# HGRN operand sums moved to the first head's levels 0 and 1, and input units 4 and 5 run as a tenth pair

## The chip, the cores and the metric

One core of a Trainium2 chip runs the kernel. The metric is the device time of one execution in microseconds (us), told as the median of several. TensorE, VectorE (DVE in the profile), ScalarE (ACT), GpSimd (POOL) and SyncE (SP) run their own instruction streams and meet at semaphores.

## The reference

The reference is two blocks in a row on x of 1024 tokens by 1024. The part around the change is the first block's HGRN2 mixer:

```python
h = _rmsnorm(x, norm_mix[layer])
proj = h @ w_in                          # 1024 x 4096: q, f, i, g
q, f, i, g = jnp.split(proj, 4, axis=-1)
log_f = jnp.logaddexp(jnp.log(lb), jnp.log1p(-lb) + jax.nn.log_sigmoid(ff))
k = (1.0 - lb) * jax.nn.sigmoid(-ff)
qf = jax.nn.silu(q.astype(jnp.float32)) * (HGRN_HEAD_DIM ** -0.5)
o = _hgrn2_chunk_scan(heads(qf), heads(k), heads(i.astype(jnp.float32)), heads(log_f))
o = o * lax.rsqrt(jnp.mean(o * o, axis=-1, keepdims=True) + NORM_EPS)
```

The scan has 8 heads of 128. An output projection, a squared-relu MLP (1024 to 4096 and back), a second block with retention and a convolution, and a second MLP follow. All in float32.

## The kernel before, in words

Each matrix product in float32 is made of three fp32r matmuls: weights and activations are both split into a rounded high part and a low rest, and hi x hi, hi x lo and lo x hi are added (`tiles`, L1052 to L1054; 128x512 each). A *unit* is 128 output columns of a projection, for 1024 tokens in two halves; a plain unit is 2 halves x 8 k-tiles x 3 = 48 matmuls. Head n owns units 3n (v), 3n+1 (f, later k) and 3n+2 (q). The weights of a unit (512 KB) come through one of two slots of `w_raw`; SP loads the next unit into a slot once `w_split` says the slot's last low part is made.

From unit 6 on two units run as a *pair* (`paired`): one Strassen-Winograd step over the first four k-tiles. Seven products of 6 matmuls (P1, P5, P2, S2xT2, S4xB22, S3xT3, A22xT4) and four plain rests of 12 over k-tiles 4 to 7 make 90 matmuls. The operand sums T1, T3, T2, T4 of the activations serve all pairs of the stage: VectorE makes each (`in1_combine`, L2296, two instructions), ACT rounds it (`in1_high`, L3232), VectorE makes the low part (`in1_low`, L2303). For the weights of a pair ACT rounds the raw upper half (`in_high_raw`, L3151), POOL adds S1 and S2 (L926, L928), ACT rounds them (`in_high_s12`, L3157), POOL makes low parts (`split_paired`, L910, counted by `in1_parts`), rounds and splits the rest tiles (L914, L917), and adds S3 and S4; ACT rounds these (`in_high_more`). ACT copies P1, P5 and the partial sums U2, U3 from PSUM (`in_copy`, L3128), and VectorE adds them to the banks (L1933, L1920). A table of PSUM banks (`PAIR_BANKS1`) says in which of four banks each pair works, and with it which eviction each product waits for. TensorE's first product of a pair waits for `in1_parts`:

```python
                part(1)
                free(n_u)
                seventh(b_u, A11, B11, True).then_inc(s.prod, 1)
                part(3)
```

Between the pieces of a unit or pair TensorE does the side work of the heads ahead (`hgrn_steps`). For the head before the current units it makes levels L0 to L6, and for the one before that L7, the turns of v and k, the states and the output. A level goes around three engines: VectorE multiplies q and k by the decay (`grow`, L2079, with the next decay L2080) once TensorE has made that level, and takes the scores (L2103); ACT mixes q and k into one operand for the next level (`gather`, L3175, L3176); TensorE multiplies (L1192). The key turn (L1111, second use) waits for level 7's multiply and for its scores.

The order on every engine is written by hand: `hgrn_iteration` on VectorE, `second_iteration`, `even_iteration` and `odd_iteration` on ACT, the calls at the end of POOL's part. In iteration 1 (units 3 to 5, head 0's levels) VectorE makes the four operand sums after levels 2 to 5 and the low parts after level 5 and at the end; ACT rounds the first pair's weights after it has mixed for level 6.

## Time and profile before

| what | value |
|---|---|
| median of 3 runs | 2258.19 us (2257.88 to 2261.65) |
| the profiled execution | 2260.37 us |
| its span, first to last instruction | 2258.6 us |
| TensorE busy, matmuls | 2244.6 us, 99% of the span |
| VectorE busy | 1682.2 us, 74% |
| POOL busy | 1256.8 us, 56% |
| ACT busy | 951.9 us, 42% |
| mean granted TensorE clock | 0.998 |
| HBM traffic | 121 GB/s over the span |

A timeline row gives the start and the length of an instruction; matmuls overlap, so their pace is the distance of their starts. "[idle before <-releaser]" is how long the engine had stood still, and what it waited for.

### The profile page before, as it was taken

How to read it: one execution, taken by the hardware profiler on the slowest of the kernel's cores; microseconds unless marked ns; L12 is line 12 of the kernel's file. 1: busy time of each engine (PE TensorE's matmuls, PEld its weight loads, DVE VectorE, ACT ScalarE, POOL GpSimd, SP SyncE). 2: the span in 40 equal slices, each digit the busy share in tenths (PEclk: the TensorE clock that was granted, in tenths of full speed). 3: DMA queues.
4: the chain of work that ended last, by engine and by line, in shares of the span. 5: the costliest groups of instructions: out<-in, count | busy, mean ns of one | idle time of the engine just before them, and what ended most of it. 6: DMA issues, size and time to landing. Idle time of an engine off the chain costs nothing.

```text
span 2258.6 us, 32472 instructions
## 1 busy us (share of the span) xinstructions
PE 2244.6 (99%) x10744; PEld 1879.4 (83%) x10744; DVE 1682.2 (74%) x2355; ACT 951.9 (42%) x1565; POOL 1256.8 (56%) x1420
## 2 busy tenths in 40 slices
PE   9999999999999999999999999999999999999998
PEld 7888888888888888888888888888888888888887
DVE  7887887856878777876666877765787787787766
ACT  6355544424634533543432224322453454344433
POOL 4544552344556566655546666763556665666562
PEclk9999999999999999999999999999999999999999
DMA  4011111023264556455313111112335645554553
GB/s 158 29 38 38 33 34 47 29 93 130 94 229 144 180 173 214 149 177 187 114 55 121 66 43 41 48 56 103 121 136 181 214 148 177 186 198 142 196 198 140
DMA packets 60020, 274.46 MB, mean 122 GB/s; under 512 B 7184, under 2 KB 10384, under 8 KB 42000
## 3 DMA queue, kind: packets, MB, share of 16 engines
q1 hardware_dynamic: 58800, 270.51, 34.5%
q10 hardware_dynamic: 1120, 2.65, 0.3%
q8 instruction: 58, 0.95, 0.2%
q14 instruction: 42, 0.34, 0.0%
HBM read 211.27 MB, written 61.87 MB: 121 GB/s over the span
## 4 chain that ended last, share of the span: by engine, by line
PE 95%; DVE 3%; DVEq 1%; ACT 0%; issue 0%; DMA 0%; SPq 0%; ACTq 0%; POOL 0%; POOLq 0%
PE prod_ps L1466 8%; PE prod_ps L1467 8%; PE prod_ps L1468 8%; PE side_ps L1467 7%; PE side_ps L1468 7%; PE side_ps L1466 7%; PE prod_ps L1052 7%; PE prod_ps L1054 7%; PE prod_ps L1053 7%; PE prod_ps L1343 3%; PE prod_ps L1345 3%; PE prod_ps L1344 3%; PE prod_ps L1333 3%; PE prod_ps L1331 3%; PE prod_ps L1332 3%; PE side_ps L1192 2%
## 5 line engine op out<-in xcount | busy, mean ns | idle before, releaser
L1052 PE MATMUL prod_ps<-operand_hi,w_hi 128*128 128x512 f32 x696 | 275.3, 396 | 2.1 <-DVE operand_lo L1971 2.1
L1054 PE MATMUL prod_ps<-operand_hi,w_lo 128*128 128x512 f32 x696 | 271.8, 391 | 0.0
L1053 PE MATMUL prod_ps<-operand_lo,w_hi 128*128 128x512 f32 x696 | 271.4, 390 | 0.0
L842 POOL TENSOR_TENSOR w_lo<-w_raw,w_hi 128x256 fp32r<-128x256 f32 x168 | 154.8, 941 | 127.4 <-ACT w_hi L3410 127.1
L842 POOL TENSOR_TENSOR w_lo<-w_s,w_hi 128x256 fp32r<-128x256 f32 x168 | 129.0, 771 | 143.0 <-ACT w_more_hi L3418 115.1
L797 POOL CAST w_hi<-w_raw 128x1024 fp32r<-128x1024 f32 x41 | 43.6, 1064 | 266.6 <-PE prod_ps L1054 177.2
L2491 DVE TENSOR_TENSOR x_res<-prod_ps,x_res 128x512 f32<-128x512 f32 x130 | 89.0, 685 | 97.6 <-PE prod_ps L1468 97.6
L801 POOL TENSOR_TENSOR w_lo<-w_raw,w_hi 128x256 fp32r<-128x256 f32 x164 | 155.5, 979 | 3.3
L1052 PEld LDWEIGHTS prod_ps<-operand_hi,w_hi 128*128 128x128 f32 x696 | 131.1, 188 | 29.1 <-DVE operand_lo L1971 2.4
L1054 PEld LDWEIGHTS prod_ps<-operand_hi,w_lo 128*128 128x128 f32 x696 | 130.9, 188 | 27.9
L1053 PEld LDWEIGHTS prod_ps<-operand_lo,w_hi 128*128 128x128 f32 x696 | 131.2, 189 | 26.2
L3410 ACT ACTIVATE w_hi<-w_raw 128x512 fp32r<-128x512 f32 x114 | 70.7, 628 | 184.2 <-PE side_ps L1468 78.7
L2491 DVE TENSOR_TENSOR x_res<-side_ps,x_res 128x512 f32<-128x512 f32 x182 | 122.5, 684 | 27.4 <-PE side_ps L1468 23.3
L3414 ACT ACTIVATE w_hi<-w_s 128x512 fp32r<-128x512 f32 x114 | 72.0, 632 | 166.4 <-DVE w_s L2375 166.4
L1343 PE MATMUL prod_ps<-operand_hi,w_hi 128*128 128x512 f32 x320 | 128.4, 401 | 0.0
L1345 PE MATMUL prod_ps<-operand_hi,w_lo 128*128 128x512 f32 x320 | 125.8, 393 | 0.0
L1344 PE MATMUL prod_ps<-operand_lo,w_hi 128*128 128x512 f32 x320 | 125.4, 392 | 0.0
L842 POOL TENSOR_TENSOR w_s_lo<-w_s,w_more_hi 128x256 fp32r<-128x256 f32 x168 | 123.7, 757 | 0.0
L2476 DVE TENSOR_TENSOR wino_lo<-wino,wino_hi 128x1024 fp32r<-128x1024 f32 x78 | 109.0, 1410 | 11.3 <-ACT wino_hi L3481 9.3
L3418 ACT ACTIVATE w_more_hi<-w_s 128x512 fp32r<-128x512 f32 x114 | 71.9, 633 | 83.7 <-DVE w_s L2385 83.7
L842 POOL TENSOR_TENSOR w_a_lo<-w_raw,w_more_hi 128x256 fp32r<-128x256 f32 x84 | 67.4, 803 | 38.1 <-ACT w_more_hi L3421 38.1
L2375 DVE TENSOR_TENSOR w_s<-w_s,w_raw 128x256 f32<-128x256 f32 x114 | 79.3, 695 | 8.5
(461 smaller groups left out, 6842.8 us busy)
## 6 DMA issues: line engine op xcount, KB each, us to landing
w_raw<-stream SPq DMA_DIRECT2D x202, 512.0 KB, 3.6
x_park<-x_res SPq DMA_DIRECT2D x45, 1024.0 KB, 8.1
x_res<-x_park SPq DMA_DIRECT2D x45, 1024.0 KB, 6.8
swapped<-op_park SPq DMA_DIRECT2D x39, 1024.0 KB, 5.0
op_park<-swapped SPq DMA_DIRECT2D x6, 1024.0 KB, 8.2
x_in<-x_t SPq DMA_DIRECT2D x16, 256.0 KB, 5.2
x_res<-x_t SPq DMA_DIRECT2D x8, 512.0 KB, 4.3
end_park<-x_res SPq DMA_DIRECT2D x4, 1024.0 KB, 3.8
```

The lines of the kernel that those rows point to most:

```text
L801: low = nc.gpsimd.tensor_tensor(w_lo[:, slot, ks], w_raw[:, slot, ks], w_hi[:, slot, ks].bitcast(F32), ALU.subtract)
L842: return nc.gpsimd.tensor_tensor(dst, src, high.bitcast(F32), ALU.subtract)
L1052: nc.tensor.matmul(into, w_h, a_h, start=(k == 0), stop=False)
L1053: nc.tensor.matmul(into, w_h, a_l, start=False, stop=False)
L1054: last = nc.tensor.matmul(into, w_l, a_h, start=False, stop=(k == KT - 1))
L1343: nc.tensor.matmul(into, w_h, a_h, start=first, stop=False, skip_group_check=not start)
L1344: nc.tensor.matmul(into, w_h, a_l, start=False, stop=False, skip_group_check=not start)
L1345: mm = nc.tensor.matmul(into, w_l, a_h, start=False, stop=k == KT - 1, skip_group_check=not start)
L1466: nc.tensor.matmul(into, w_h, a_h, start=first and kk == 0, stop=False, skip_group_check=not first)
L1467: nc.tensor.matmul(into, w_h, a_l, start=False, stop=False, skip_group_check=not first)
L1468: mm = nc.tensor.matmul(into, w_l, a_h, start=False, stop=kk == 1, skip_group_check=not first)
L2491: nc.vector.tensor_tensor(x_res[:, m, tokens(half)], src, x_res[:, m, tokens(half)], ALU.add).then_inc(down_taken, 1)
```

## The change

`U_PAIRED1` goes from `U_IN1 + 6` to `U_IN1 + 4`: units 4 and 5 become pair 0 and there are ten pairs. The bank table gets other last entries. On TensorE iteration 1 is now `second_head`: unit 3 as two plain halves, followed by L0 and L1, then the new pair with L2 to L6 between its pieces. VectorE makes all four sums between level 0 and level 1, the low parts directly behind level 1, and takes level 6's scores ahead of its multiply. ACT has a new order for this iteration, and the first copies of the later heads' iterations lose their special case. POOL no longer splits units 4 and 5 singly.

```diff
-U_PAIRED1 = U_IN1 + 6
+U_PAIRED1 = U_IN1 + 4
-PAIR_BANKS1, PAIR_FREED1 = pair_banks(U_PAIRED1, IN1_PAIRS, [(0, 1, 3, 2), (1, 3, 2, 0), (3, 2, 0, 1)])
+PAIR_BANKS1, PAIR_FREED1 = pair_banks(U_PAIRED1, IN1_PAIRS, [(1, 0, 2, 3), (3, 2, 0, 1)])
...
-            split_units(4, U_PAIRED1)
...
+                if n == 1:
+                    mids = [None, None, lambda: newer_level(2), lambda: newer_level(3), None, None]
+                    ends = [lambda: newer_level(0), lambda: newer_level(1), None, lambda: newer_level(4),
+                            lambda: newer_level(5), lambda: newer_level(6)]
+                elif n >= HEADS1 or n < 1:
...
+            def second_head():
+                mids, ends = hgrn_steps(1, 1)
+                for half in range(NH):
+                    product(3, 1, half, 0, mid=mids[half])
+                    ends[half]()
+                in1_pair(0, mids[2:6], ends[2:6])
...
-                    scores_first = number == LEVELS - 2 and 2 <= n < HEADS1
+                    scores_first = number == LEVELS - 2 and 1 <= n < HEADS1
...
+                if n == 1:
+                    newer_level(0)
+                    in1_combine(T1, 0, 1, T1)
+                    group(0)
+                    in1_combine(T3, 2, 1, T3)
...
+                    newer_level(1)
+                    in1_low(T1, 1)
+                    group(1)
...
+                    newer_level(5)
+                    group(4)
+                    group(5)
+                    newer_level(6)
+                    second(4)
+                    second(5)
+                    return
...
             def second_iteration():
                 newer_gather(1, 1)
+                in1_high(T1, 1)
+                in1_high(T3, 2)
+                in1_high(T2, 3)
                 newer_gather(1, 2)
...
                 in_high_raw(in1, 0)
                 in_high_s12(in1, 0)
...
+                newer_gather(1, 4)
+                f_sigmoids(1, 1)
+                in_high_raw(in1, 1)
+                in_high_s12(in1, 1)
+                newer_gather(1, 5)
+                copy_u3(in1, 0)
+                q_sigmoid(1, 0)
+                newer_gather(1, 6)
```

VectorE, from level 0's scores of head 0 on, before (`in_t_200`, `_206`, `_203`, `_207` are T1, T3, T2, T4; `hgrn_kq_78` is head 0's keys and queries, `_79` head 1's):

```order
L2091 TENSOR_TENSOR hgrn_scores_80<-side_ps,ident 128x1024
L1957 TENSOR_TENSOR hgrn_v_t_77<-prod_ps,inv_rms 128x512 [waits prod]
L2079 TENSOR_TENSOR hgrn_kq_78<-hgrn_kq_78,hgrn_f 128x2x512 [waits side_done]
L2080 TENSOR_TENSOR hgrn_decay_83<-hgrn_f 128x512
L2103 COPY_PREDICATED hgrn_scores_80<-masks,side_ps 128x4x64 x2
L1957 TENSOR_TENSOR hgrn_v_t_77<-prod_ps,inv_rms 128x512 [waits prod]
L2079 TENSOR_TENSOR hgrn_kq_78<-hgrn_kq_78,hgrn_decay_83 128x2x256x2 [waits side_done]
L2080 TENSOR_TENSOR hgrn_decay_84<-hgrn_decay_83 128x256
L2103 COPY_PREDICATED hgrn_scores_80<-masks,side_ps 128x4x32x2 x2
```

and with the change:

```order
L2103 TENSOR_TENSOR hgrn_scores_80<-side_ps,ident 128x1024
L2321 SCALAR_TENSOR_TENSOR in_t_200<-x_in,gain,in_t_200 128x512 [waits in1_scaled]
L2321 SCALAR_TENSOR_TENSOR in_t_200<-x_in,gain,in_t_200 128x512
L1969 TENSOR_TENSOR hgrn_v_t_77<-prod_ps,inv_rms 128x512 [waits prod]
L2321 SCALAR_TENSOR_TENSOR in_t_206<-x_in,gain,in_t_206 128x512 x2
L2321 SCALAR_TENSOR_TENSOR in_t_203<-x_in,gain,in_t_200 128x512 x2
L2321 SCALAR_TENSOR_TENSOR in_t_207<-x_in,gain,in_t_203 128x512 x2
L2091 TENSOR_TENSOR hgrn_kq_78<-hgrn_kq_78,hgrn_f 128x2x512 [waits side_done]
L2092 TENSOR_TENSOR hgrn_decay_83<-hgrn_f 128x512
L2115 COPY_PREDICATED hgrn_scores_80<-masks,side_ps 128x4x64 x2
L2328 TENSOR_TENSOR in_t_lo<-in_t_200,in_t_hi 128x1024 [waits in1_t_high]
```

The four sums now stand between level 0's scores and level 1's multiply (`hgrn_kq_78<-hgrn_kq_78,hgrn_f 128x2x512`), which came directly behind the v eviction before.

ACT, from the first rounding of a sum to the roundings of the first pair's weights (`w_hi<-w_raw`, `w_hi<-w_s`) before; `hgrn_mixed` rows are two per level, and the ones for levels 4 and 5 (`16x16`, `8x32`) and 6 are told apart by their shapes:

```order
L3232 ACTIVATE in_t_hi<-in_t_200 128x1024 [waits in1_t_made]
L3175 ACTIVATE hgrn_mixed<-hgrn_kq_78 128x16x16 [waits level_fed]
L3176 ACTIVATE hgrn_mixed<-hgrn_kq_78 128x16x16
L3221 ACTIVATE hgrn_f<-hgrn_kq_79 128x512 [waits evac]
L3222 ACTIVATE hgrn_kq_79<-hgrn_kq_79 128x2x2x128
L3224 ACTIVATE hgrn_f<-hgrn_f,lb 128x512
L3232 ACTIVATE in_t_hi<-in_t_206 128x1024 [waits in1_t_made]
L3175 ACTIVATE hgrn_mixed<-hgrn_kq_78 128x8x32 [waits level_fed]
L3176 ACTIVATE hgrn_mixed<-hgrn_kq_78 128x8x32
L3151 ACTIVATE w_hi<-w_raw 128x512 [waits prod,w_landed0]
L3157 ACTIVATE w_hi<-w_s_0_121 128x512 [waits in1_sum]
L3232 ACTIVATE in_t_hi<-in_t_203 128x1024 [waits in1_t_made]
```

and with the change, from the mixing for level 1 on:

```order
L3200 ACTIVATE hgrn_mixed<-hgrn_kq_78 128x256 [waits level_fed]
L3201 ACTIVATE hgrn_mixed<-hgrn_kq_78 128x256
L3257 ACTIVATE in_t_hi<-in_t_200 128x1024 [waits in1_t_made]
L3257 ACTIVATE in_t_hi<-in_t_206 128x1024 [waits in1_t_made]
L3257 ACTIVATE in_t_hi<-in_t_203 128x1024 [waits in1_t_made]
L3200 ACTIVATE hgrn_mixed<-hgrn_kq_78 128x128x2 [waits level_fed]
L3201 ACTIVATE hgrn_mixed<-hgrn_kq_78 128x128x2
L3176 ACTIVATE w_hi<-w_raw 128x512 [waits prod,w_landed0]
L3182 ACTIVATE w_hi<-w_s_0_121 128x512 [waits in1_sum]
L3257 ACTIVATE operand_hi<-in_t_207 128x2x512 [waits in1_t_made,prod]
L3153 ACTIVATE in_c_213<-prod_ps 128x512 [waits in1_prod]
```

The first pair's weights are now rounded behind the mixing for level 2 (`128x128x2`) instead of behind that for level 6 (`8x32`), and that mixing stands behind the rounding of three sums.

## Rows read from the trace of the kernel before

**Rows 1.** The page: its first line and the busy times.

```profile
span 2258.6 us, 32472 instructions
...
PE 2244.6 (99%) x10744; PEld 1879.4 (83%) x10744; DVE 1682.2 (74%) x2355; ACT 951.9 (42%) x1565; POOL 1256.8 (56%) x1420
```

**Rows 2.** Waits of TensorE over the whole span, the longest.

```profile
PE side_ps L1111 <- DVE hgrn_scores L2103: 2.1, 1, 2.1
```

**Rows 3.** Timeline of TensorE: start us, us, engine, line, operation [idle before <-releaser].

```profile
42.49 0.39 PE L1054 MATMUL prod_ps<-operand_hi,w_lo 128*128 128x512 f32 x1
...
50.65 0.40 PE L1054 MATMUL prod_ps<-operand_hi,w_lo 128*128 128x512 f32 x1
...
58.98 0.48 PE L1052 MATMUL prod_ps<-operand_hi,w_hi 128*128 128x512 f32 x1
```

**Rows 4.** Timeline of TensorE around the key turn of head 0.

```profile
99.58 0.96 PE L1111 MATMUL side_ps<-ident,hgrn_kq 128*128 128x128 f32 x7 [2.15 <-DVE hgrn_scores L2103]
...
100.61 0.63 PE L1344 MATMUL prod_ps<-operand_lo,w_hi 128*128 128x512 f32 x1
...
104.02 0.39 PE L1343 MATMUL prod_ps<-operand_hi,w_hi 128*128 128x512 f32 x1
```

**Rows 5.** Windows: busy us of each engine, PEclk, DMA share, GB/s.

```profile
8.60:12.00 3.40, 3.32 (x8) 2.65 (x9) 2.75 (x5) 2.85 (x6) 3.32 (x4) 0.52 1.08 395
...
100.00:104.00 4.00, 4.00 (x14) 3.21 (x13) 3.34 (x4) 1.76 (x5) 2.20 (x4) 0.57 0.72 232
```

**Rows 6.** Timeline of TensorE near the start.

```profile
8.68 0.80 PE L1052 MATMUL prod_ps<-operand_hi,w_hi 128*128 128x512 f32 x1 [1.93 <-DVE operand_lo L1971]
...
11.83 0.40 PE L1053 MATMUL prod_ps<-operand_lo,w_hi 128*128 128x512 f32 x1
```

**Rows 7.** Timeline of VectorE.

```profile
54.01 1.22 DVE L2091 TENSOR_TENSOR hgrn_scores<-side_ps,ident 128x1024 f32<-128x1024 f32 x1
...
59.26 1.33 DVE L2079 TENSOR_TENSOR hgrn_kq<-hgrn_kq,hgrn_f 128x1024 f32<-128x1024 f32 x1 [3.25 <-PE side_ps L1192]
...
67.48 1.41 DVE L2296 SCALAR_TENSOR_TENSOR in_t<-x_in,gain,in_t 128x512 f32<-128x512 f32 x2
...
71.68 1.89 DVE L2296 SCALAR_TENSOR_TENSOR in_t<-x_in,gain,in_t 128x512 f32<-128x512 f32 x2
...
80.72 0.78 DVE L2103 COPY_PREDICATED hgrn_scores<-masks,side_ps 128x256 f32<-128x256 uint8 x2
...
94.56 1.75 DVE L2303 TENSOR_TENSOR operand_lo<-in_t,operand_hi 128x1024 fp32r<-128x1024 f32 x1
...
96.23 1.76 DVE L2079 TENSOR_TENSOR hgrn_kq<-hgrn_kq,hgrn_decay 128x1024 f32<-128x1024 f32 x1
...
99.60 0.69 DVE L1933 TENSOR_TENSOR in_c<-prod_ps,in_c 128x512 f32<-128x512 f32 x1 [0.16 <-issue]
```

**Rows 8.** Timeline of ACT.

```profile
60.63 0.44 ACT L3175 ACTIVATE hgrn_mixed<-hgrn_kq 128x256 f32<-128x256 f32 x1 [5.74 <-DVE hgrn_kq L2079]
...
60.97 0.43 ACT L3176 ACTIVATE hgrn_mixed<-hgrn_kq 128x256 f32<-128x256 f32 x1
...
67.60 0.64 ACT L3221 ACTIVATE hgrn_f<-hgrn_kq 128x512 f32<-128x512 f32 x1 [1.78 <-DVE hgrn_kq L2136]
...
68.82 0.82 ACT L3224 ACTIVATE hgrn_f<-hgrn_f,lb 128x512 f32<-128x512 f32 x1
...
81.21 0.61 ACT L3151 ACTIVATE w_hi<-w_raw 128x512 fp32r<-128x512 f32 x1
...
83.20 0.61 ACT L3213 ACTIVATE sig<-hgrn_kq 128x512 f32<-128x512 f32 x1
```

**Rows 9.** Timeline of POOL.

```profile
58.48 1.04 POOL L797 CAST w_hi<-w_raw 128x1024 fp32r<-128x1024 f32 x1 [8.15 <-issue]
...
81.90 1.89 POOL L910 TENSOR_TENSOR w_lo<-w_raw,w_hi 128x256 fp32r<-128x256 f32 x2 [7.74 <-ACT w_hi L3151]
```

**Rows 10.** The page, section 6: loads of weights.

```profile
w_raw<-stream SPq DMA_DIRECT2D x202, 512.0 KB, 3.6
```

More of the change, by code:

```diff
@@ L1258, in sixth_level_then_back @@
                     back()
-                if n >= HEADS1 or n < 2:
+                if n == 1:
[3 more added lines that the diff above has]
+                elif n >= HEADS1 or n < 1:
                     mids = [turn_v_and_last_level, turn_k, kv_then_second_level, lambda: newer_level(3), None,
@@ L1287, in hgrn_iteration, with in1_pair @@
                         ends[j]()
+            def in1_pair(j, mids, ends):
+                m0, m1, m2, m3 = mids
+                e0, e1, e2, e3 = ends
+                paired(in1, j, {"P2": m0, "c11": e0, "P6": m1, "c12": e1, "P7": m2, "c22": e2, "P4": m3, "c21": e3})
+            def second_head():
[4 more added lines that the diff above has]
+                in1_pair(0, mids[2:6], ends[2:6])
             def two_heads(n):
@@ L1293, in two_heads @@
                 for p in range(3):
-                    m0, m1, m2, m3 = mids[4 * p:4 * p + 4]
-                    e0, e1, e2, e3 = ends[4 * p:4 * p + 4]
-                    paired(in1, (3 * n - U_PAIRED1) // 2 + p,
-                           {"P2": m0, "c11": e0, "P6": m1, "c12": e1, "P7": m2, "c22": e2, "P4": m3, "c21": e3})
+                    in1_pair((3 * n - U_PAIRED1) // 2 + p, mids[4 * p:4 * p + 4], ends[4 * p:4 * p + 4])
             def in_weight(s, which, kk):
@@ L1440, in _ @@
             hgrn_iteration(0, 0, mid_start=True)
-            hgrn_iteration(1, 1)
+            second_head()
             for n in range(2, HEADS1, 2):
@@ L2178, in first_pair_of @@
                     first_two(in1, (unit - U_PAIRED1) // 2)
+                if n == 1:
[3 more added lines that the diff above has]
+                    in1_combine(T3, 2, 1, T3)
+                    dve.drain()
+                    in1_combine(T2, 2, 1, T1)
+                    dve.drain()
+                    in1_combine(T4, 2, 0, T2)
+                    newer_level(1)
+                    in1_low(T1, 1)
+                    group(1)
+                    in1_low(T2, 3)
+                    in1_low(T3, 3)
+                    in1_low(T4, 4)
+                    newer_level(2)
+                    group(2)
+                    newer_level(3)
+                    first_pair_of(u + 1)
+                    group(3)
+                    newer_level(4)
+                    newer_level(5)
[5 more added lines that the diff above has]
+                    return
                 if 2 <= n < HEADS1:
@@ L2285, in hgrn_iteration @@
                 second(5)
-                if n == 1:
-                    in1_low(T2, 3)
-                    in1_low(T3, 3)
-                    in1_low(T4, 4)
             def in1_combine(op, m, half, other):
@@ L3255, in second_iteration @@
                 newer_gather(1, 1)
+                in1_high(T1, 1)
+                in1_high(T3, 2)
+                in1_high(T2, 3)
                 newer_gather(1, 2)
-                newer_gather(1, 3)
-                f_sigmoids(1, 0)
-                newer_gather(1, 4)
-                in1_high(T1, 1)
-                newer_gather(1, 5)
-                f_sigmoids(1, 1)
-                in1_high(T3, 2)
-                newer_gather(1, 6)
                 in_high_raw(in1, 0)
                 in_high_s12(in1, 0)
-                in1_high(T2, 3)
-                q_sigmoid(1, 0)
-                newer_gather(1, LEVELS - 1)
-                q_sigmoid(1, 1)
-                take_v(2)
                 act.wait_ge(prod, 2 * U_PAIRED1)
                 in1_high(T4, 4)
+                copy_p1(in1, 0)
+                copy_p5(in1, 0)
+                newer_gather(1, 3)
+                in_high_more(in1, 0)
+                f_sigmoids(1, 0)
+                copy_u2(in1, 0)
+                newer_gather(1, 4)
[6 more added lines that the diff above has]
+                newer_gather(1, 6)
+                in_high_more(in1, 1)
+                q_sigmoid(1, 1)
+                newer_gather(1, LEVELS - 1)
             def even_iteration(n, j):
@@ L3277, in even_iteration @@
                 copy_p5(in1, j)
-                if n > 2:
-                    take_v(n)
-                else:
-                    in_high_more(in1, j)
+                take_v(n)
                 in_high_raw(in1, j + 1)
@@ L3340, in _ @@
             for n in range(2, HEADS1, 2):
-                even_iteration(n, 3 * (n // 2 - 1))
-                odd_iteration(n + 1, 3 * (n // 2 - 1) + 2)
+                even_iteration(n, 3 * (n // 2) - 2)
+                odd_iteration(n + 1, 3 * (n // 2))
             def gate_sigmoid(j):
```

11 lines of the change are left out of this document (removed).

## The prediction

> **What bounds the kernel now.** I read the page first: TensorE is busy for 2244.6 of 2258.6 us [rows 1]. So the time is TensorE's instruction stream plus its few gaps, and a gap of a few us anywhere reaches the end whole. The view of the waits names the largest gap: 2.1 us, once [rows 2]. TensorE's timeline gives the rest. Its pace: 36 matmuls of 512 columns from 42.49 to 50.65 us, 0.2267 us each; unit 4 starts at 58.98 [rows 3]. The gap: it ends at 99.58, where the key turn (k) inside the first pair waits for VectorE. After it, eight matmuls from 100.61 to 104.02 take 0.426 us each [rows 4], and the windows give a granted clock of 0.57 from 100 to 104 us: the 1.2 GHz level [rows 5]. They cost 3.41 - 8 x 0.2267 = 1.6 us on top of the gap. The same had followed a gap of 1.93 us at 8.68 [rows 6], with a clock of 0.52 [rows 5]. So a gap of some 2 us costs nearly twice its length here.
>
> A change is told from no change on this kernel only beyond 0.2%, 4.5 us. Everything below happens before 110 us; behind that the pairs follow one another as before.
>
> **The change, part by part.**
>
> *Fewer matmuls.* Units 4 and 5 took 4 halves x 8 tiles x 3 = 96 matmuls; a pair takes 7 products x 6 + 4 x 12 = 90. Six go: -6 x 0.2267 = **-1.4 us**. Level products (L1, L2, ...) and turns keep their number.
>
> *The first weights of the new pair come late.* This is the term that decides. TensorE's first product P1 needs w_lo, which POOL makes behind the ACT rounding w_hi<-w_raw. In ACT's new order that rounding stands behind the mixing for level 2, which waits for VectorE's level-1 multiply (the kq grow, L2079 before). In VectorE's new order this multiply stands behind all four operand sums. Link by link: VectorE is done with level 0 at 55.23. Then four sums of two instructions, 1.41 us each while POOL idles, and one eviction of 0.69: 6.3 us end on end, some 0.3 less as neighbours overlap by 0.07, 0.2 more for two drains: 61.5. The multiply takes 1.33 [rows 7]: 62.8. ACT mixes in 0.77 (60.63 to 61.40) and rounds in 0.61 [rows 8]: 64.2. POOL's first low part takes 0.95, half of 1.89 [rows 9]: **65.2**. TensorE wants it at 58.98, so it waits **6.2 us**. Before, the same split was covered by two units of matmuls. The least this can be is VectorE having finished the sums in 5.3 us (eight instructions spaced 0.6, plus the eviction): 5.5; the most is contention on the sums, below: 8.2.
>
> VectorE's sums cost 1.41 a pair with POOL idle and 1.89 with POOL at work (67.48 against 71.68) [rows 7]. By the Trainium skill, GPSIMD Engine Reference, section Specifications, the two engines share their SBUF interfaces, and VectorE instructions with two SBUF inputs contend; these sums are such. If that held here too, they would take 7.6 instead of 5.6, and this term would be 8.2. POOL stood idle for 8.15 us up to 58.48 [rows 9]; now its queue waits at the first low part from about 48 until 64.2, so I take 6.2.
>
> *The clock behind that gap.* A gap three times as long as the two seen surely leaves TensorE at the half clock. The two stretches after a restart were 3.15 us (8.68 to 11.83, seven matmuls) [rows 6] and 3.41 us after 0.7 us of turns. Half of such a stretch is lost: 1.6 at least; the restart may fall early between two changes and cost up to twice that, 3.3. I take **+2.0**; the first 0.4 of it covers the wait for the third weight part (POOL: two more low parts behind the first, 67.0), which I therefore don't add.
>
> *Two small waits further in.* With P1 at 65.3, TensorE would reach the third product's end about 81.2, L5 at 81.2 + 0.9 (L4) + 18 x 0.2267 = 86.2. L5 needs its mixing, which on ACT stands behind the sigmoids of unit 4's second half and the next pair's two roundings: eviction on VectorE 2 x 0.7 to 83.0, sigmoids 2.04 (67.60 to 69.64), roundings 1.15, mixing 0.8 [rows 7, 8]: 87.0. Wait **0.8**. L6 is wanted 4.1 us (18 matmuls) after L5. It needs: VectorE's level-5 multiply 1.23 to 1.75, decay and scores 1.0, an eviction in two steps 1.57, ACT's q sigmoid 0.61 (now ahead of that mixing) and the mixing 0.8: 5.5 with the drains. Wait **1.4**. Both are bounded below by 0 (other work earlier than I put it) and above by 1.8 and 2.0 (POOL beside VectorE all the way: 0.5 more for each multiply). L3 and L4 are ready 0.4 to 0.7 early by the same count. Between the first and last link I take 2.2 together.
>
> *The old gap goes.* It came from VectorE: three low parts of the operand sums, the last at 94.56, stood ahead of the level-7 multiply (96.23), whose scores the turn waits for [rows 2, 7]. These now come about 25 us earlier. By my count level 7's scores end 3 us before the turn is reached. -2.2 for the gap, -1.6 for its half clock: **-3.8 us**.
>
> *What I cost at nothing.* The single split of units 4 and 5 leaves POOL (5 instructions each, off the path). Four ACT copies at 0.55 us and four VectorE additions at 0.69 to 1.1 are added; they lie beside matmuls, save those counted for L5 and L6. The load of unit 6 now waits for the pair's last low part, about 79.7, and needs 3.6 [rows 10]: 83.3, ahead of its rounding at 85.1; were that cover gone, L5 would be late by the difference. The new bank table lets the first product of the last two pairs wait for the second eviction of the pair ahead where it waited for the third, and no wait stood there: 0.
>
> Sum: -1.4 + 6.2 + 2.0 + 2.2 - 3.8 = **+5.2 us**. The profiled execution took 2260.37 for its span of 2258.6; it would take 2265.6. The median of the runs shown is 2258.19, 2.2 lower, so I forecast 2263.4.
>
> **The rivals.**
>
> 1. *The small waits trip the clock as well.* L6's 1.4 us follows L5's 0.8. For it: 1.93 us sufficed at 8.68. Against: no wait of 0.5 to 1.4 in this trace is followed by slow matmuls. Another +1.6: 2265.0. Chance 0.2.
> 2. *The late waits are covered.* Should ACT or VectorE be earlier than I count, or the clock be back soon, the two small waits fall to 0: 5.2 - 2.2 = +3.0, 2261.2, inside what counts as no change. For it: the slow matmuls after P1 give the other engines slack. Against: both chains start from TensorE's own progress and so move with it. Chance 0.22.
> 3. *The first weights are in time* (the other side). Should the rounding reach POOL by 58, the change is -1.4 - 3.8 = -5.2 us: 2253.0, faster by 0.23%. It decides at the P1 chain: its 6.2 us must shrink under 0.7 for a gain of 4.5. Against: the level-1 multiply alone waits for L1, that ends after 58.98, and 1.33 + 0.77 + 0.61 + 0.95 follow it, so 3.7 us remain even with no sum ahead. It needs my reading of ACT's order to be wrong. Chance 0.04.
> 4. *The old gap stays.* If VectorE is still behind at level 7, the -3.8 is missing: +9.0, 2267.2. For it: L6's scores, its multiply and the q scaling now all lie close ahead of level 7. Against: 3 us of slack. Chance 0.05.
> 5. *POOL contends with the sums or the multiplies:* +2 us, 2265.4. Chance 0.07.
>
> **How the numbers follow.** The forecast keeps 0.42, with its own range of +4.0 to +6.6 from the clock term (1.6 to 3.3) and the first chain (5.5 upward); about 0.3 of its 0.42 lies above 4.5. Slower by over 0.2%: 0.3 + 0.2 + 0.05 + 0.07 = 0.62. Within: 0.12 + 0.22 = 0.34. Faster: 0.04. The range runs from 2260.5 (rival 2 with a cheap restart) to 2267.2 (rival 4), leaving out rival 3 and the tails.
>
> **What would show it.** In the profile after: a gap of about 6 us on TensorE ahead of the first paired product, released by POOL's w_lo, from about 59 to 65; 0.43 us a matmul for some 4 us behind it; gaps near 1 us at the fifth and sixth levels of the first head, released by ACT's mixing; no wait at the first key turn, and full pace behind it. The pair behind the new one would start about 94, against 85.5. I am wrong if P1 starts before 62, if TensorE is at full clock right behind it, or if a new wait shows in a later pair.

## The result, and the profile after

The changed kernel takes 2271.14 us (median of 6 runs, 2269.64 to 2271.74); the kernel before, run beside it, 2259.04 (6 runs, 2257.6 to 2261.65). The ratio is 1.005, 95% interval 1.0039 to 1.0061: slower, by more than twice the 5.2 us that were forecast, and above the range given. The profiled execution took 2269.92 us. Of all executions told of in this document one, of 5870.88 us (in e12), was disturbed; without it that median moves by 0.01 us.

The page of the changed kernel, its first line and the busy times:

```profile
span 2268.1 us, 32491 instructions
...
PE 2246.6 (99%) x10738; PEld 1877.4 (83%) x10738; DVE 1684.0 (74%) x2359; ACT 955.9 (42%) x1573; POOL 1264.3 (56%) x1427
```

Against [rows 1] six matmuls are gone (x10738), and still TensorE is busy 2.0 us longer: a matmul at half clock counts as busy for its whole, longer time. Its waits (us in total, times, longest):

```profile
PE prod_ps L1343 <- POOL w_lo L910: 6.3, 2, 5.8
PE side_ps L1191 <- ACT hgrn_mixed L3201: 2.5, 2, 1.9
...
PE prod_ps L1478 <- ACT stage L3518: 1.4, 2, 0.9
```

The wait of [rows 2] is not in the list. The timeline of TensorE from L0 of head 0 (`x16`) to L0 of head 2, with L1, P1, P5, L2, L3, L5, L6, the matmuls behind L6, and the key turn:

```profile
49.98 1.95 PE L1104 MATMUL side_ps<-hgrn_kq 128*128 128x128 f32 x16
...
57.22 1.07 PE L1191 MATMUL side_ps<-hgrn_kq,hgrn_mixed 128*128 128x128 f32 x8
64.07 0.79 PE L1343 MATMUL prod_ps<-operand_hi,w_hi 128*128 128x512 f32 x1 [5.79 <-POOL w_lo L910]
...
67.56 0.50 PE L1343 MATMUL prod_ps<-in_t_hi,w_hi 128*128 128x512 f32 x1 [0.56 <-POOL w_lo L910]
...
70.45 1.07 PE L1191 MATMUL side_ps<-hgrn_kq,hgrn_mixed 128*128 128x128 f32 x8
...
76.23 1.05 PE L1191 MATMUL side_ps<-hgrn_kq,hgrn_mixed 128*128 128x128 f32 x8
...
87.01 1.16 PE L1191 MATMUL side_ps<-hgrn_kq,hgrn_mixed 128*128 128x128 f32 x8 [0.61 <-ACT hgrn_mixed L3201]
...
94.21 1.88 PE L1191 MATMUL side_ps<-hgrn_kq,hgrn_mixed 128*128 128x128 f32 x8 [1.91 <-ACT hgrn_mixed L3201]
95.74 0.77 PE L1343 MATMUL prod_ps<-operand_hi,w_hi 128*128 128x512 f32 x1
...
97.95 0.39 PE L1345 MATMUL prod_ps<-operand_hi,w_lo 128*128 128x512 f32 x1
...
108.58 0.93 PE L1110 MATMUL side_ps<-ident,hgrn_kq 128*128 128x128 f32 x7
...
153.04 1.95 PE L1104 MATMUL side_ps<-hgrn_kq 128*128 128x128 f32 x16
```

The key turn at 108.58 has no gap [rows 4]. P1 waited 5.79 us. L6 waited 1.91, and its eight matmuls took 1.88 in place of 1.05: the clock had fallen there too, as the windows show (PEclk is the third number from the right):

```profile
65.00:70.00 5.00, 4.44 (x16) 2.99 (x15) 5.00 (x5) 1.19 (x2) 4.92 (x4) 0.79 0.00 0
...
95.00:100.00 5.00, 5.00 (x21) 4.23 (x20) 3.75 (x6) 1.98 (x5) 4.71 (x6) 0.71 0.34 103
```

The chain of the first weights, on VectorE, ACT and POOL in turn:

```profile
56.35 4.41 DVE L2321 SCALAR_TENSOR_TENSOR in_t<-x_in,gain,in_t 128x512 f32<-128x512 f32 x6
60.68 1.22 DVE L2091 TENSOR_TENSOR hgrn_kq<-hgrn_kq,hgrn_f 128x1024 f32<-128x1024 f32 x1
```

```profile
62.59 0.61 ACT L3176 ACTIVATE w_hi<-w_raw 128x512 fp32r<-128x512 f32 x1
```

```profile
63.28 2.50 POOL L910 TENSOR_TENSOR w_lo<-w_raw,w_hi 128x256 fp32r<-128x256 f32 x2 [16.81 <-ACT w_hi L3176]
```

This run started 0.9 us earlier (L0 at 49.98, before at 50.88), so these rows are the forecast chain of 61.5, 62.8, 64.2 and 65.2, less 0.9, to within 0.3.

**Two stretches hold the whole difference.** From L0 of head 0 to L0 of head 2 the kernel before took 145.58 - 50.88 = 94.70 us, the changed one 153.04 - 49.98 = 103.06: **+8.4**, forecast +5.2. From there to the last sums of `x_res` on VectorE it is 2105.45 before (2251.03) and 2107.50 after (2260.54): **+2.05**, forecast 0. Inside the second stretch, the kernel before, VectorE and then TensorE in the second MLP:

```profile
1648.94 0.43 DVE L2373 TENSOR_TENSOR w_s<-w_raw 128x256 f32<-128x256 f32 x1 [0.20 <-PE prod_ps L1654]
1649.44 0.43 DVE L2375 TENSOR_TENSOR w_s<-w_s,w_raw 128x256 f32<-128x256 f32 x1
```

```profile
1673.91 0.49 PE L1466 MATMUL prod_ps<-xop_hi,w_hi 128*128 128x512 f32 x1 [0.48 <-ACT stage L3489]
```

and the changed kernel:

```profile
1656.49 0.42 DVE L2398 TENSOR_TENSOR w_s<-w_raw 128x256 f32<-128x256 f32 x1 [0.20 <-PE prod_ps L1666]
1657.34 0.94 DVE L2400 TENSOR_TENSOR w_s<-w_s,w_raw 128x256 f32<-128x256 f32 x1 [0.43 <-issue]
```

```profile
1682.33 0.49 PE L1478 MATMUL prod_ps<-xop_hi,w_hi 128*128 128x512 f32 x1 [0.93 <-ACT stage L3518]
```

VectorE halts for 0.43 us on nothing that the profile shows, the next sum takes 0.94 in place of 0.43, and TensorE's wait at 1682 us is 0.45 longer. No instruction of the change is near.

### The profile page after: what moved, and what is told of

Read it like the earlier page. It is cut to its first block, busy times and chain, and to the rows that moved or that the text cites. A ratio compares the mean times of both kernels' runs of the same rounds, so it can differ in the third digit from the quotient of the medians.

```text
span 2268.1 us, 32491 instructions
## 1 busy us (share of the span) xinstructions
PE 2246.6 (99%) x10738; PEld 1877.4 (83%) x10738; DVE 1684.0 (74%) x2359; ACT 955.9 (42%) x1573; POOL 1264.3 (56%) x1427
## 4 chain that ended last, share of the span: by engine, by line
PE 93%; DVE 3%; DVEq 1%; ACT 1%; issue 1%; SPq 0%; DMA 0%; POOL 0%; ACTq 0%
PE prod_ps L1478 8%; PE prod_ps L1480 8%; PE prod_ps L1479 8%; PE side_ps L1478 7%; PE side_ps L1480 7%; PE side_ps L1479 7%; PE prod_ps L1051 6%; PE prod_ps L1053 6%; PE prod_ps L1052 6%; PE prod_ps L1355 3%; PE prod_ps L1357 3%; PE prod_ps L1356 3%; PE prod_ps L1343 3%; PE prod_ps L1345 3%; PE prod_ps L1344 3%; PE side_ps L1191 2%
## 5 line engine op out<-in xcount | busy, mean ns | idle before, releaser
L1051 PE MATMUL prod_ps<-operand_hi,w_hi 128*128 128x512 f32 x664 | 261.9, 394 | 1.2 <-DVE operand_lo L1983 1.0
L1053 PE MATMUL prod_ps<-operand_hi,w_lo 128*128 128x512 f32 x664 | 258.9, 390 | 0.0
L1052 PE MATMUL prod_ps<-operand_lo,w_hi 128*128 128x512 f32 x664 | 258.4, 389 | 0.0
L842 POOL TENSOR_TENSOR w_lo<-w_raw,w_hi 128x256 fp32r<-128x256 f32 x168 | 154.3, 938 | 128.7 <-ACT w_hi L3439 128.4
L801 POOL TENSOR_TENSOR w_lo<-w_raw,w_hi 128x256 fp32r<-128x256 f32 x156 | 147.9, 978 | 3.1
L1051 PEld LDWEIGHTS prod_ps<-operand_hi,w_hi 128*128 128x128 f32 x664 | 124.7, 188 | 28.0 <-POOL w_lo L995 1.4
L1053 PEld LDWEIGHTS prod_ps<-operand_hi,w_lo 128*128 128x128 f32 x664 | 124.6, 188 | 26.5
L1052 PEld LDWEIGHTS prod_ps<-operand_lo,w_hi 128*128 128x128 f32 x664 | 124.8, 188 | 24.9
L1355 PE MATMUL prod_ps<-operand_hi,w_hi 128*128 128x512 f32 x336 | 134.3, 400 | 0.0
L1357 PE MATMUL prod_ps<-operand_hi,w_lo 128*128 128x512 f32 x336 | 131.4, 391 | 0.0
L1356 PE MATMUL prod_ps<-operand_lo,w_hi 128*128 128x512 f32 x336 | 130.9, 390 | 0.0
L926 POOL TENSOR_TENSOR w_s<-w_raw 128x256 f32<-128x256 f32 x21 | 16.8, 802 | 125.1 <-PE prod_ps L1345 117.2
```

Of the source, the lines that this page charges most:

```text
L801: low = nc.gpsimd.tensor_tensor(w_lo[:, slot, ks], w_raw[:, slot, ks], w_hi[:, slot, ks].bitcast(F32), ALU.subtract)
L842: return nc.gpsimd.tensor_tensor(dst, src, high.bitcast(F32), ALU.subtract)
L1051: nc.tensor.matmul(into, w_h, a_h, start=(k == 0), stop=False)
L1052: nc.tensor.matmul(into, w_h, a_l, start=False, stop=False)
L1053: last = nc.tensor.matmul(into, w_l, a_h, start=False, stop=(k == KT - 1))
L1355: nc.tensor.matmul(into, w_h, a_h, start=first, stop=False, skip_group_check=not start)
```

## The experiments

Called "head" is the stretch from L0 of head 0 to L0 of head 2, "far" the one from there to the last `x_res` sums; "ratio" is to the kernel before, run beside each; it comes from all the times, so it is not always the quotient of the two medians.

**e1, first weights ahead of the mixing for level 2.** Theory A: the gap at P1 is the chain sums, multiply, mixing, rounding, low part.

```diff
             def second_iteration():
+                in_high_raw(in1, 0)
+                in_high_s12(in1, 0)
                 newer_gather(1, 1)
...
-                in_high_raw(in1, 0)
-                in_high_s12(in1, 0)
```

> The changed kernel with ACT's two roundings of the new pair's weights moved ahead of the mixing for level 1, nothing else. Theory A (the gap is a VectorE chain, and the weights are only its first victim): P1 starts at once, but its second product P5 then waits for T1's low part, which VectorE makes behind level 1. In the changed kernel that low part ended at 65.2 and P5 began at 67.56, so the gap moves to P5, stays near 5.5 us, and 2.3 us come off: about 2268.8. Rival B (the late weights are the whole cause): the gap of 5.8, the 0.56 behind it and the half clock of 1.3 to 2 all go, 7.7 to 8.4 us less: about 2263.

Measured: 2272.12 us, ratio 1.0055 (1.0039 to 1.007). P1 has no gap, the second product has it all, and VectorE's six sums take 5.83 us in place of 4.41, since POOL now works beside them. TensorE, then VectorE:

```profile
69.26 0.77 PE L1343 MATMUL prod_ps<-in_t_hi,w_hi 128*128 128x512 f32 x1 [8.25 <-DVE in_t_lo L2328]
```

```profile
57.80 5.83 DVE L2321 SCALAR_TENSOR_TENSOR in_t<-x_in,gain,in_t 128x512 f32<-128x512 f32 x6
63.55 1.74 DVE L2091 TENSOR_TENSOR hgrn_kq<-hgrn_kq,hgrn_f 128x1024 f32<-128x1024 f32 x1
```

ACT's order does set P1's gap, but VectorE's low part of T1 stands right behind it. That is theory A in kind and not in size: the gap grew to 8.25 where 5.5 was expected, and the time did not fall. By the Trainium skill, GPSIMD Engine Reference, section Specifications, POOL contends on the SBUF interfaces with VectorE's instructions of two SBUF inputs; the trace agrees: POOL works from 58.78 us on, each sum takes 0.47 us more, and the multiply 1.74 in place of 1.22.

**e2, all three engines reordered** (T1, T2 and T1's low part ahead of level 1, T3 later, T4's low part on POOL, ACT in the order of need):

```diff
-                    in1_combine(T3, 2, 1, T3)
                     dve.drain()
                     in1_combine(T2, 2, 1, T1)
                     dve.drain()
-                    in1_combine(T4, 2, 0, T2)
+                    in1_low(T1, 1)
                     newer_level(1)
-                    in1_low(T1, 1)
+                    in1_combine(T4, 2, 0, T2)
+                    dve.drain()
+                    in1_low(T2, 2)
                     group(1)
...
```

> The changed kernel with its orders rebuilt: T1, T2 and T1's low part ahead of level 1, T4, T2's low part and T3 behind it, T4's low part on POOL, the weights' roundings first on ACT, mixings ahead of roundings and sigmoids. Theory A (all of the loss is order, none is the pair itself): at most a wait of 0.8 before L3 and 1.1 before S3xT3 stay; relative to the kernel before -1.4 - 3.8 + 1.9 = -3.3 us, about 2255.7. Rival B (ten pairs cost by themselves in head 1, whatever the order): a gap over 3 us stays in the new pair and the time stays above that of the kernel before, 2259 to 2262.

Measured: 2268.47 us, ratio 1.0039 (1.0025 to 1.0053), head 102.29. No gap at P1; instead five: 1.52 at S2xT2, 0.77 and 1.19 at L3 and L4, 1.07 at S3xT3, and the largest at A22xT4, where I had put ACT's copy of U3 behind two roundings:

```profile
90.79 0.79 PE L1350 MATMUL prod_ps<-operand_hi,in_more_hi 128*128 128x512 f32 x1 [4.10 <-ACT in_c L3163]
```

Theory A is out, and rival B came true, with a time above its 2259 to 2262.

**e3, the two later mixings first.**

```diff
-                in_high_raw(in1, 1)
-                in_high_s12(in1, 1)
                 newer_gather(1, 5)
+                in_high_raw(in1, 1)
+                in_high_s12(in1, 1)
                 copy_u3(in1, 0)
-                q_sigmoid(1, 0)
                 newer_gather(1, 6)
+                q_sigmoid(1, 0)
```

> The changed kernel with ACT's mixing for level 5 ahead of the next pair's two roundings and the mixing for level 6 ahead of the q sigmoid. Theory A: the waits before L5 (0.61) and L6 (1.91) go, and with the latter the slow matmuls behind it (1.7, eight level matmuls and five of 512 columns): -4.2 us, about 2267, clock 1.00 from 95 to 100. Rival B (the clock behind L6 is a late echo of the 6 us gap, not of the 1.9 us one): the waits go, 2.5 us, but 95 to 100 stays slow: about 2268.6.

Measured: 2266.10 us, ratio 1.0028 (1.0018 to 1.0039), head 100.10. L5 and L6 start without a wait, all is at full clock behind them, and P1's gap is unchanged:

```profile
65.23 0.79 PE L1343 MATMUL prod_ps<-operand_hi,w_hi 128*128 128x512 f32 x1 [5.79 <-POOL w_lo L910]
...
68.71 0.80 PE L1343 MATMUL prod_ps<-in_t_hi,w_hi 128*128 128x512 f32 x1 [0.56 <-POOL w_lo L910]
...
94.13 1.05 PE L1191 MATMUL side_ps<-hgrn_kq,hgrn_mixed 128*128 128x128 f32 x8
```

The small waits and what followed them were worth 5.0 us by the medians, not 2.2. The head stretch alone would say 3.0, since this trace lost more elsewhere: behind the same wait of 5.79 us, 15 matmuls were slow (P5 took 0.80 in place of 0.50), and from L1 to L2 it took 15.13 us where the changed kernel's trace has 13.23.

**e4, the kernel before with T3's and T4's low parts behind level 7.**

```diff
                 if n == 1:
                     in1_low(T2, 3)
-                    in1_low(T3, 3)
-                    in1_low(T4, 4)
...
                     level(par, LEVELS - 1)
+                    if n == 2:
+                        in1_low(T3, 3)
+                        in1_low(T4, 4)
```

(Level 0 of the next head goes ahead of the first eviction there.)

> The kernel before, without the tenth pair: the low parts of T3 and T4 moved behind head 0's level 7 on VectorE, and level 0 of head 1 ahead of the eviction of v. Theory A (the old gap is these low parts, and its half clock costs as much again): the gap of 2.15 at the key turn and the 1.6 behind it go, -3.8 us, about 2255.2. Rival B (the half clock behind it is not due to the gap): only -2.15, about 2256.9. Rival C (the parts are merely late elsewhere): a wait at S3xT3 takes the place, no change.

Measured: 2257.88 us, ratio 0.9995 (0.9986 to 1.0004), head 92.45. The old gap and its slow matmuls are gone, and a new wait shows at L3 of head 1:

```profile
115.40 1.16 PE L1192 MATMUL side_ps<-hgrn_kq,hgrn_mixed 128*128 128x128 f32 x8 [1.29 <-ACT hgrn_mixed L3181]
```

**e5, the kernel before with 11 more drains on VectorE at the start.** Theory B for the far loss: it comes from where VectorE's instructions lie in its stream.

```diff
                 nc.vector.tensor_tensor(gain[:, G_END1_MIX2], gain[:, G_END1], gain[:, G_MIX2], ALU.mult)
-                dve.drain()
+                for _ in range(12):
+                    dve.drain()
```

> The kernel before with 11 more drains on VectorE among the masks and gains made at the start, far off the path; VectorE's stream gets as long as in the changed kernel (2571 instructions in place of 2560), and nothing else differs. Theory B (the loss of 1.2 to 2.1 us behind the first head, in the second MLP, comes from where VectorE's instructions lie in its stream, not from the pair): the VectorE row pair that takes 0.94 us in place of 0.43 near 1650 us shows here too, the later wait of TensorE at L1466 behind it is 0.9 in place of 0.5 us, and the time is 1.2 to 2.1 us above that of the kernel before, ratio 1.0005 to 1.001. Rival (it comes from the ten pairs themselves, by their banks or the later state of the queues): the stretch from the first head to the end is as in the kernel before, within 0.3 us, ratio 1.000.

Measured: 2261.61 us against 2260.16, ratio 1.0005 (0.9996 to 1.0014), which does not separate them. The trace does: head 94.87, as before, and far 2107.07 (before 2105.45, after 2107.50), with the same halt, then the same wait, and a second halt at 2153.88 us:

```profile
1649.04 0.43 DVE L2374 TENSOR_TENSOR w_s<-w_raw 128x256 f32<-128x256 f32 x1 [0.20 <-PE prod_ps L1654]
1649.89 0.94 DVE L2376 TENSOR_TENSOR w_s<-w_s,w_raw 128x256 f32<-128x256 f32 x1 [0.42 <-issue]
...
2153.88 0.98 DVE L2386 TENSOR_TENSOR w_s<-w_raw,w_s 128x256 f32<-128x256 f32 x1 [0.45 <-issue]
```

```profile
1674.90 0.49 PE L1466 MATMUL prod_ps<-xop_hi,w_hi 128*128 128x512 f32 x1 [0.92 <-ACT stage L3490]
```

These two places hold nearly all of it. Matmul by matmul, TensorE here runs 0.11 us behind the kernel before at 1645 us and 1.01 behind at 1676, then 1.04 at 2152 and 1.62 at 2156. The changed kernel and e3 lose the same two amounts there, 0.85 to 0.9 and 0.6.

**e6, e3 with 5 more drains there** (the same edit to `range(6)`).

> As e3 (ten pairs, the mixings for levels 5 and 6 ahead of the roundings), with 5 more drains on VectorE at the start, far off the path: its stream then has 2576 instructions, 16 more than the kernel before, where e3 has 11 more. e5 showed that 11 drains alone cost 1.6 us behind the first head. Theory B in its narrow form (what counts is where the pair of w_s rows lies within a block of 16 instructions of the stream): the rows near 1650 us take 0.43 us again, the wait behind them 0.5, and the stretch from the first head's end to the last instruction falls back from 2108.4 to about 2107, so the time is 1.2 to 1.5 us under e3's 2266.1. Rival (any added instruction, or another period): the rows stay at 0.94 us or another place is hit, 2108 to 2109 for the stretch, and the time is e3's.

Measured: 2265.75 us, ratio 1.0027 (1.0016 to 1.0039). Far is 2105.70, as before the change (e3: 2106.88), and the halt now meets an instruction three rows earlier:

```profile
1651.48 0.69 DVE L2497 SCALAR_TENSOR_TENSOR stage<-stage,side_ps 128x512 f32<-128x512 f32 x1 [0.43 <-issue]
...
1653.22 0.42 DVE L2399 TENSOR_TENSOR w_s<-w_raw 128x256 f32<-128x256 f32 x1
1653.72 0.43 DVE L2401 TENSOR_TENSOR w_s<-w_s,w_raw 128x256 f32<-128x256 f32 x1
```

Neither place near 1650 nor near 2155 costs TensorE more than 0.12 us now. Two things did not come out as the expectation had them. Its block of 16 instructions is not borne out: the stream is 16 longer than before, yet the halts don't come back to the lines that they met before. And the median is only 0.35 under e3's, where the stretch gains 1.2: the two ran in different batches, and over the fourteen traces L0 starts anywhere from 49.98 to 52.55 us.

**e7, e2 with ACT's copy of U3 ahead of two roundings.**

```diff
                 newer_gather(1, 5)
+                copy_u3(in1, 0)
                 f_sigmoids(1, 1)
                 in_high_raw(in1, 1)
                 in_high_s12(in1, 1)
-                copy_u3(in1, 0)
```

> As e2, but ACT copies U3 of the new pair right behind the mixing for level 5, ahead of the f sigmoids and of the next pair's two roundings. Theory C (ten pairs can be fed, e2 lost its time at one copy that stood too far back): the wait of 4.1 us at A22xT4 goes, with the slow matmuls behind it (1.6 us), and the waits of 1.1 to 1.5 us ahead of it stay: e2's 2268.5 less 4.1 to 5.7, so 2262.8 to 2264.4, ratio 1.0015 to 1.0025. Theory D (the pair is starved by VectorE's and ACT's queues as a whole, so a wait that is removed comes back one product later): above 2266, with a new wait of over 2 us between L5 and L7. Under neither is it below the kernel before by more than 0.2%.

Measured: 2267.02 us, ratio 1.0028 (1.0018 to 1.0038), head 99.81. The wait of 4.1 is gone, and one of 2.16 stands at L6:

```profile
97.81 1.87 PE L1198 MATMUL side_ps<-hgrn_kq,hgrn_mixed 128*128 128x128 f32 x8 [2.16 <-ACT hgrn_mixed L3211]
```

That is theory D: a wait that is removed comes back later. No single run tells whether the queues of VectorE and ACT as a whole are the reason, as the theory has it.

**e8, e4 with the states of head 0 behind level 2's multiply and decay of head 1.**

```diff
                     if not scores_first:
                         grow(b, number)
+                    if n == 2 and number == 2:
+                        states()
```

> As e4 (nine pairs, the low parts of T3 and T4 behind level 7, level 0's multiply of the next head ahead of a group), and VectorE scales the states of the head between level 2's multiply with its decay and level 2's scores, not ahead of the multiply. In e4 the multiply for level 2 of head 1 stood behind the states, and TensorE waited 1.29 us at L3. Theory: that wait goes or falls under 0.5 us and no other takes its place; the old gap's 2.1 and its half clock's 1.6 us then show as a gain: 3.0 to 3.8 below the kernel before, 2255 to 2256, ratio 0.9983 to 0.9987. Rival: the states are then late for the output turns, a wait of 0.5 to 1.5 us shows there, and the time is that of e4, 2257.9.

Measured: 2260.73 us, ratio 1.0001 (0.9992 to 1.001), head 94.73. Neither came true. L3 works in the PSUM banks that held the products for the states, and these come free only when VectorE has made the states, now later. VectorE, then TensorE:

```profile
114.08 2.46 DVE L2172 SCALAR_TENSOR_TENSOR hgrn_state<-hgrn_state,hgrn_decay,side_ps 128x128 f32<-128x128 f32 x6
116.67 1.31 DVE L2105 COPY_PREDICATED hgrn_scores<-masks,side_ps 128x256 f32<-128x256 uint8 x2
```

```profile
116.68 1.73 PE L1192 MATMUL side_ps<-hgrn_kq,hgrn_mixed 128*128 128x128 f32 x8 [2.02 <-DVE hgrn_state L2172]
```

The states end at 116.54 and L3 starts at 116.68, with the half clock behind it (1.73 for its eight matmuls).

**e9, e3 with only T1's sum ahead of level 1.**

```diff
                     in1_combine(T1, 0, 1, T1)
                     group(0)
+                    newer_level(1)
                     in1_combine(T3, 2, 1, T3)
-                    dve.drain()
                     in1_combine(T2, 2, 1, T1)
                     dve.drain()
+                    in1_low(T1, 1)
                     in1_combine(T4, 2, 0, T2)
-                    newer_level(1)
-                    in1_low(T1, 1)
+                    dve.drain()
```

(ACT rounds T3 and T2 behind the first weights.)

> As e3 (the changed kernel with the mixings for levels 5 and 6 ahead of the roundings of the next pair and of the q sigmoid), and only the sum T1 stays ahead of level 1's multiply on VectorE; T3, T2 and T4 follow it, and ACT rounds T3 and T2 behind the first weights. Theory A (the gap ahead of P1 is VectorE's chain of eight sum instructions ahead of the multiply): the multiply comes as soon as TensorE has made level 1 and VectorE has evicted v, 3 to 4 us earlier, the gap ahead of P1 falls from 5.8 to 2.5 to 3.5 us; P2, S2xT2 and their low parts may be 0.5 to 2 us late. Sum: 2.5 to 3.3 less than e3's 2266.1 at best, 2263 to 2265. Rival: the gap only moves, as in e1: T2's and T3's operands are then late for S2xT2 and S3xT3 by as much as P1 gains, and the time stays at 2266.

Measured: 2267.81 us, ratio 1.0034 (1.0022 to 1.0046), head 100.27, as e3. P1's gap falls to 3.44, and the second product waits the rest:

```profile
62.42 0.79 PE L1343 MATMUL prod_ps<-operand_hi,w_hi 128*128 128x512 f32 x1 [3.44 <-POOL w_lo L910]
68.71 0.76 PE L1343 MATMUL prod_ps<-in_t_hi,w_hi 128*128 128x512 f32 x1 [3.36 <-DVE in_t_lo L2328]
```

The rival again. With e1 and e7 this is the third order in which the gap only moves. My reading, which no run isolates: at 59 us VectorE has the operand work of the pair still ahead of it, and TensorE's order leaves it nothing else to do.

**e10, nine pairs, each sum and low part one place earlier.**

```diff
                 newer_level(0)
                 group(0)
+                if n == 1:
+                    in1_combine(T1, 0, 1, T1)
                 newer_level(1)
...
                         group(0)
                         newer_level(0)
+                        if n == 2:
+                            in1_low(T4, 4)
```

(T3, T2 and T4 follow where T1, T3 and T2 were summed, the low parts of T1 and T2 ahead of level 6, T3's ahead of level 7; ACT rounds a place earlier.)

> Nine pairs as in the kernel before; of the change only its idea that the operand sums come earlier: the sum T1 goes into VectorE's idle 3.25 us between levels 0 and 1, each other sum and low part moves one place up, and T4's low part stands behind level 0's scores of the next head; ACT rounds T1, T3 and T2 a place earlier. VectorE's stream keeps its length. Theory (the old gap at the key turn came from three low parts ahead of level 7's multiply, and VectorE had the room to make them earlier): level 7's scores end about 97 us, the gap of 2.15 us and the half clock behind it (1.6) go, no wait over 0.4 us takes their place, since the states and level 2 of the next head are not displaced as in e4: 3.3 to 3.8 us below the kernel before, ratio 0.9983 to 0.9986. Rival (VectorE is full from level 5 of head 0 to level 3 of head 1, so that any order leaves a wait of 1 to 1.3 us at L3 as in e4): 2 to 2.5 us below at best, ratio 0.999 to 1.0.

Measured: 2257.15 us, ratio 0.9991 (0.9982 to 1.0), head 90.94 (3.76 less than before), far 2105.54. The sum fills VectorE's idle time, the key turn has no gap, and L3 of head 1 waits 0.23. By the trace that is the theory; the medians lie only 2.8 apart, under its 3.3 to 3.8:

```profile
55.26 1.41 DVE L2298 SCALAR_TENSOR_TENSOR in_t<-x_in,gain,in_t 128x512 f32<-128x512 f32 x2
```

```profile
96.61 0.93 PE L1111 MATMUL side_ps<-ident,hgrn_kq 128*128 128x128 f32 x7
...
113.55 1.16 PE L1192 MATMUL side_ps<-hgrn_kq,hgrn_mixed 128*128 128x128 f32 x8 [0.23 <-ACT hgrn_mixed L3178]
```

**e11 and e12, the changed kernel and e10 again, unedited.**

> The changed kernel again, unedited, for a second trace and more times. The account so far: from L0 of head 0 to L0 of head 2 it takes 103.1 us where the kernel before takes 94.7, and 2 us more from there to the end, 10.4 in all; the medians lay 12.1 apart. If the account is complete, this run's two stretches are 103.1 and 2107.5 again within 0.5 us, and its median is 10 to 11 us above that of the kernel before run beside it, ratio 1.0045 to 1.005. Rival (a part of the loss is a state of the chip that the one trace missed, as a second lost stretch of the clock): the median is again 12 us above, ratio 1.0053 or more, and the second trace shows slow matmuls that the first has not.

> The kernel of e10 again, unedited, to narrow its interval. Its trace was 3.76 us shorter than the kernel before between L0 of head 0 and L0 of head 2 and equal behind that, but its times lay only 2.8 us lower by the median, with an interval up to 1.0. If the trace is the rule: the same stretch takes 90.9 us again within 0.3, and the ratio is 0.9983 to 0.9990 with an interval below 1. Rival (the start and the clock near it eat a part of the gain in most runs): ratio 0.9990 to 1.0.

Measured, e11: 2271.09 us against 2260.31, ratio 1.0045 (1.0032 to 1.0059), head 102.05, far 2107.15. L6 waited as long as in the first trace, and this time the clock stayed up:

```profile
95.45 1.16 PE L1191 MATMUL side_ps<-hgrn_kq,hgrn_mixed 128*128 128x128 f32 x8 [1.92 <-ACT hgrn_mixed L3201]
96.36 0.47 PE L1343 MATMUL prod_ps<-operand_hi,w_hi 128*128 128x512 f32 x1
```

In exchange the slow stretch behind P1 was longer (12 matmuls, where the first trace has 6), and L5 waited 1.24. The median and the far stretch are as expected; the head is 1.0 shorter than expected. e12: 2257.37 us, ratio 0.9988 (0.9978 to 0.9997), head 91.94, far 2106.11; L3 of head 1 waited 1.03 here, so that the head is 1.0 longer than expected. e10's kernel is thus faster than the kernel before by 2.8 and 2.9 us of median, within what counts as no change; its gain in the head, 3.76 and 2.76, is what was forecast as -3.8.

## Why the prediction was wrong, step by step

The sign was right, and so was the kind of each term that was counted. Three things that were put at nothing were not nothing: the far stretch, the clock behind L6, and L2 to L4. The miss of the difference is 12.1 - 5.2 = 6.9 us: 3.2 in the head, 2.05 far, and 1.7 that the one trace does not hold. Taken apart by the distances of TensorE's starts, full pace being 5.0 us from one level product to the next in the new pair:

| step | forecast | first trace | second (e11) |
|---|---|---|---|
| six matmuls fewer | -1.4 | -1.4 | -1.4 |
| first weights late | +6.2 | +5.8 | +5.8 |
| half clock behind it, to L2 | +2.0 | +2.4 | +2.9 |
| L2 to L4 | 0 | +0.8 | +0.1 |
| L4 to L5 | +0.8 | +0.7 | +1.5 |
| L5 to L6 | +1.4 | +2.2 | +2.2 |
| L6 to the v turn | 0 | +1.7 | +0.1 |
| old gap and its half clock | -3.8 | -3.8 | -3.8 |
| sum, head | +5.2 | +8.4 | +7.4 |
| far | 0 | +2.05 | +1.7 |

- **"The first weights of the new pair come late"**: right, link by link. The first sum took 1.41 us with POOL idle, as taken, and the other three 4.41 together. The lower bound of the term took instructions spaced 0.6 us, which no row has; these six are spaced 0.73. e1 and e9 add what I had missed: shortening this chain does not pay, as the next product's operand is as late.
- **"The clock behind that gap"**: within its bounds of 1.6 to 3.3 in both traces of the changed kernel, and in e6 (2.6); in e3, behind the same wait of 5.79 us, it was 4.3. The upper bound was too low.
- **L2 to L4**, put at nothing because L3 and L4 would be ready early, cost 0.8 in the first trace and 0.1 in the second. The rows name no engine for it (0.28 "issue" at S2xT2); the cause stays open.
- **"Two small waits further in"** failed in size. L6's wait was 1.9 in place of 1.4, and 0.3 went at the restart. The missing 0.5 lies ahead of the eviction: from the end of the level-5 multiply (88.21 + 1.43) to the eviction at 91.30 the decay, the scores and the steps between took 1.7 us where I had 1.0. The eviction in two steps took 1.58, as forecast (1.57), and ACT's sigmoid started right behind it:

```profile
89.56 0.72 DVE L2092 TENSOR_TENSOR hgrn_decay<-hgrn_decay 128x32 f32<-128x32 f32 x1
...
91.30 0.69 DVE L1945 TENSOR_TENSOR in_c<-prod_ps,in_c 128x512 f32<-128x512 f32 x1 [0.16 <-issue]
92.09 0.79 DVE L2148 TENSOR_TENSOR hgrn_kq<-in_c,inv_rms 128x512 f32<-128x512 f32 x1
```

```profile
92.91 0.63 ACT L3238 ACTIVATE sig<-hgrn_kq 128x512 f32<-128x512 f32 x1 [5.47 <-DVE hgrn_kq L2148]
```

The two small waits together cost 2.9 in the first trace and 3.7 in the second, where I wrote 2.2 and bounded them by 3.8.
- **Rival 1**, that the small waits trip the clock, came true in one trace of two: 1.7 us there, as priced (1.6). It was one rival of several, with the range ending at the dearest of them, while it can come together with waits at their upper bounds (3.8 - 2.2 = 1.6). The range had to reach their sum, 5.2 + 1.6 + 1.6 = 8.4 in the head alone; that this is just what the first trace has is chance, as part of its 8.4 comes from other steps. The lower end is not clean either: rival 2's 2261.2 with the cheap restart (0.4 less) is 2260.8, not 2260.5.
- **"The old gap goes"**: right, -3.8; e10 shows 3.76 without the change in its first trace (2.76 in its second, with a wait of 1.0 at L3).
- **"Behind that the pairs follow one another as before"**, which put everything behind 110 us at nothing, failed. The pairs do; the second MLP does not, and far is 1.7 to 2.05 us longer. Neither the pair nor the bank table does it, but 11 more instructions on VectorE: e5 makes a loss of 1.6 with none of the change, e6 takes 1.2 of e3's 1.4 back with all of it. Over fourteen traces the far stretch is 2105.45, 2105.62, 2105.70, 2105.58 and 2105.54 where the stream is as long as before or 16 longer (2106.11 in e12, which fell 0.5 behind between 770 and 790 us, where VectorE waited 0.5 longer for a load of weights), and 2106.66 to 2107.61 in the eight with 11 more.
- **The level**: the forecast went down by 2.2 us to the median of three runs, 2258.19. With 6 to 28 runs that median was 2259.04 to 2260.31. Against the run beside it, 2259.04, this makes 0.9 us of the miss in the time itself (2271.14 against 2263.4).
- Ten pairs were the wrong place to look for the gain: all six orders of them stayed at 2265.75 us or above, and the gain from earlier sums is to be had with nine. That no order of ten can do it is not shown.

What stays open is where the unprofiled executions lose more. The medians lie 12.1 and 10.8 us above the kernel before, and the traces hold 10.4 and 9.0. The sums close by how the profiled executions lie: the changed kernel's were 1.2 and 1.9 below their medians, the one of the kernel before 1.3 and 0.1 above, and L0 came 0.9 and 0.2 earlier. The slow stretch behind P1 differs by 1.9 us from trace to trace (e3) and may be a part of it; no run shows that.

## What to carry to other kernels

Where the engine that sets the time is full, a stage that saves it work must have its operands by then: count what the helpers still have to do at that moment, since here three reorderings only moved the wait to the next operand. Before work is moved for a large plan, put the same work into an idle stretch of the old plan: here that alone removed the old gap, with one sum put into 3.25 us of idle time and the others one place up. And rivals that can happen together belong in the range as a sum.
